# A mixture-of-experts layer tail: each row's two expert outputs ordered by expert number, the first ones loaded and added apart, and the next tile's addition ahead of a tile's norm

## The chip, the cores and the metric

The kernel runs on one core of a Trainium2 chip. The metric is device time in microseconds (us) for one execution of the whole program. The engines that matter here are PE (TensorE, matrix products), DVE (VectorE, elementwise work and statistics), ACT (ScalarE, activations, and the issuer of some DMAs), POOL (GpSimd, the issuer of the gathers and scatters) and SP (SyncE, the issuer of the weight loads).

## The reference, cut to what matters

Two layers. Each ends in a mixture of experts (MoE) over 576 rows (512 prompt rows and 64 sample rows) of width 1024, with 16 experts of which every row uses two:

```
_, idx = lax.top_k(jnp.where(in_grp, sel, NEG_INF), TOP_K)      # TOP_K = 2 experts of a row
w = jnp.take_along_axis(scores, idx, axis=-1)
w = w / w.sum(-1, keepdims=True)
combine = jnp.einsum('tk,tke->te', w, one_hot(idx, N_EXPERTS))
for e in range(N_EXPERTS):
    h = jax.nn.silu(xt @ wg[e]) * (xt @ wu[e])
    y = y + combine[:, e:e + 1] * (h @ wd[e])
...
x = layer_norm(ALPHA * x + y, ln2_g[l], ln2_b[l])               # the layer's end
```

So a row's result is the norm of ALPHA·x plus two weighted expert outputs; which of the two is added first is free.

## The kernel before, in words

The rows lie on chip as five tiles of 128 rows (the last holds 64), `x[128, 5, 1024]`. A loop runs over the two layers. In a layer PE makes the projections (helper `product`, line L1612) in four groups of five tiles, then attention and the spatial gating, the output product, and the MoE.

In the MoE, POOL gathers the rows of an expert from a copy of x in device memory (L644), PE turns and multiplies them (gate and up L1861, down L1884), ACT brings the result out of the banks (`expert_out`, L902), and POOL scatters it to `y2_rows` in device memory (`scatter`, L650), where row 2·r + j holds output j of row r. The scatters stand in the order of the experts, and POOL waits for each to land (L691) before it frees the buffer. Which output is j = 0 is set by `pick1` and `pick2` (L1463 to L1466): `pick1` marks the expert with the best score. From these two VectorE works out the slots (`slot_done`, L1484) that POOL scatters into a table (L670) before it can gather for expert 4 and later.

Weights come as units of 1 MB that SP loads into `raw` (four places) and `raw_far` (two places). Every unit is split: ACT writes its high part (`w_hi`, L423), VectorE the rest (`w_lo`, L429), and each product runs three times over them. The first four units of the next layer are split at the end of a layer.

At the end of a layer ("the tail") ACT waits until both last scatters have landed (`out_free`, L979 to L982), then loads both outputs of each row (L987, L998) into `y_rows`, four tiles of buffers. VectorE goes through the five tiles (L1574 to L1580): add output 0 (L1555), add output 1 (L1558), statistics (L1042, L1044), centre (L1176), and, once ACT has taken the square root (L994), scale and shift (L1182), which marks the tile ready (`x_ready`). In the first layer PE then turns the tile (L1601), ACT and VectorE write its high and low part (`xt_hi` L439, `xt_lo` L444), and PE starts the next layer's first projection on it (`head`, L1639). There PE turns tile t + 1 before it multiplies tile t, and its queue is in order. In the second layer SP stores the tile (L557, L559) and the program ends.

The program has a branch for experts with more than 128 rows (`overflow`); every engine reads the count and jumps past it, as no expert here has so many.

## Time and profile before

| | us |
|---|---|
| median of 3 runs (1206.41 to 1212.07) | 1209.77 |
| the profiled execution | 1211.5 |
| its span in the trace | 1210.0 |
| PE busy | 1066.1 (88%) |
| DVE busy | 904.0 (75%) |
| ACT busy | 699.5 (58%) |
| POOL busy | 188.5 (16%) |

The shares are averages. PE is the bound over most of the span, but in two stretches it stands still: between the layers (about 574 to 634 us it works only in pieces) and after 1162 us, when the last product is done and only the second layer's tail is left. The profile's page has the busy share of PE at 0 in the last of its 40 slices and at 3 tenths in the one before.

### The profile page before, as it was taken

What the parts mean: (1) busy time and instruction counts of PE and PEld (TensorE: products, weight loads), DVE (VectorE), ACT (ScalarE), POOL (GpSimd) and SP (SyncE); (2) the same over time, 40 slices, a digit from 0 to 9 for tenths busy, and PEclk for the clock granted to TensorE, in tenths of its full rate; (3) what the DMA queues carried; (4) which work ended last, traced back from release to release, by engine and by line L of the source; (5) the groups of instructions that cost most, each with busy time, mean ns of one, the idle gap of its engine ahead of it and who ended that gap; (6) DMA issues with size and microseconds to landing.
All of it is one profiled execution on the core that took longest, in us unless ns stands there. A gap on an engine that the chain in (4) does not pass through costs nothing.

```text
span 1210.0 us, 16840 instructions
## 1 busy us (share of the span) xinstructions
PE 1066.1 (88%) x5460; PEld 893.4 (74%) x5460; DVE 904.0 (75%) x1148; ACT 699.5 (58%) x851; POOL 188.5 (16%) x162
## 2 busy tenths in 40 slices
PE   5999799989989999998379988999898999999930
PEld 4987588877878888887269857887677888888820
DVE  2683865388979988886877738655898899888948
ACT  2423665265767887877223247534477888878830
POOL 3000000014522111210020000100173311011100
PEclk9999889998989999999689987999799999999975
DMA  9523101227999999996814202002589999999742
GB/s 293 165 77 105 57 32 44 87 76 275 370 335 380 388 377 380 383 381 259 301 46 155 74 32 87 27 28 95 203 288 379 351 392 391 381 382 389 304 182 83
DMA packets 115748, 273.26 MB, mean 226 GB/s; under 512 B 10144, under 2 KB 13184, under 8 KB 114528
## 3 DMA queue, kind: packets, MB, share of 16 engines
q1 hardware_dynamic: 98608, 227.36, 51.6%
q0 software_dynamic: 14464, 33.01, 7.9%
q10 hardware_dynamic: 2608, 12.06, 2.8%
q8 instruction: 33, 0.54, 0.2%
q14 instruction: 35, 0.29, 0.1%
HBM read 262.02 MB, written 25.22 MB: 237 GB/s over the span
## 4 chain that ended last, share of the span: by engine, by line
PE 55%; DMA 15%; DVE 11%; issue 6%; ACT 5%; DVEq 3%; POOL 3%; ACTq 0%; SPq 0%; POOLq 0%
DMA raw_far<-in_w_gate 10%; PE bankA L1612 9%; PE bankA L1861 8%; PE bankB L1612 7%; PE bankB L1861 6%; PE bankC L1884 4%; PE bankD L1884 4%; PE bankC L1612 4%; PE bankD L1612 4%; POOL slot_rows L670 3%; PE bankG L1685 2%; DVE w_lo L429 2%; PE bankE L1601 2%; ACT w_hi L423 2%; PE bankF L1601 1%
## 5 line engine op out<-in xcount | busy, mean ns | idle before, releaser
L429 DVE TENSOR_TENSOR w_lo<-raw,w_hi 128x2048 fp32r<-128x2048 f32 (+1 forms) x152 | 340.8, 2262 | 61.5 <-ACT w_hi L423 59.5
L423 ACT ACTIVATE w_hi<-raw 128x2048 fp32r<-128x2048 f32 (+1 forms) x152 | 287.1, 1894 | 136.5 <-PE bankC L1612 46.1
L429 DVE TENSOR_TENSOR w_lo<-raw_far,w_hi 128x2048 fp32r<-128x2048 f32 x64 | 146.5, 2288 | 13.7 <-ACT w_hi L423 13.7
L423 ACT ACTIVATE w_hi<-raw_far 128x2048 fp32r<-128x2048 f32 x64 | 122.8, 1918 | 51.0 <-PE bankB L1861 25.0
L1861 PE MATMUL bankB<-w_hi,xe_hi 128*128 128x512 f32 x256 | 103.0, 402 | 1.8 <-DVE w_lo L429 1.8
L1861 PE MATMUL bankA<-w_hi,xe_hi 128*128 128x512 f32 x256 | 102.5, 400 | 1.6 <-DVE xe_lo L444 1.3
L1861 PE MATMUL bankA<-w_lo,xe_hi 128*128 128x512 f32 x256 | 101.5, 397 | 0.0
L1861 PE MATMUL bankA<-w_hi,xe_lo 128*128 128x512 f32 x256 | 101.2, 395 | 0.0
L1861 PE MATMUL bankB<-w_hi,xe_lo 128*128 128x512 f32 x256 | 100.2, 391 | 0.0
L1861 PE MATMUL bankB<-w_lo,xe_hi 128*128 128x512 f32 x256 | 99.8, 390 | 0.0
L650 POOL DMA_INDIRECT y_rows<-expert_out,idx x32 | 47.5, 1485 | 189.6 <-ACT expert_out L902 181.1
L644 POOL DMA_INDIRECT rows<-x_rows,idx x24 | 33.4, 1393 | 223.8 <-PE bankF L1601 160.5
L1861 PEld LDWEIGHTS bankA<-w_hi,xe_hi 128*128 128x128 f32 x256 | 49.1, 192 | 14.9 <-DVE xe_lo L444 4.4
L1884 PE MATMUL bankC<-w_hi,h_hi 128*128 128x512 f32 x128 | 53.4, 417 | 4.8 <-DVE h_lo L444 4.8
L1861 PEld LDWEIGHTS bankA<-w_hi,xe_lo 128*128 128x128 f32 x256 | 49.2, 192 | 10.5
L1861 PEld LDWEIGHTS bankA<-w_lo,xe_hi 128*128 128x128 f32 x256 | 49.2, 192 | 10.0
L1861 PEld LDWEIGHTS bankB<-w_hi,xe_hi 128*128 128x128 f32 x256 | 48.1, 188 | 11.3 <-DVE w_lo L429 2.3
L1861 PEld LDWEIGHTS bankB<-w_hi,xe_lo 128*128 128x128 f32 x256 | 48.0, 188 | 10.6
L1861 PEld LDWEIGHTS bankB<-w_lo,xe_hi 128*128 128x128 f32 x256 | 48.2, 188 | 9.2
L1884 PE MATMUL bankC<-w_hi,h_lo 128*128 128x512 f32 x128 | 50.7, 396 | 0.0
L1884 PE MATMUL bankD<-w_hi,h_hi 128*128 128x512 f32 x128 | 50.6, 395 | 0.0
L1884 PE MATMUL bankC<-w_lo,h_hi 128*128 128x512 f32 x128 | 50.5, 395 | 0.0
(360 smaller groups left out, 2533.3 us busy)
## 6 DMA issues: line engine op xcount, KB each, us to landing
raw<-in_w_up SPq DMA_DIRECT2D x64, 1024.0 KB, 10.7
raw_far<-in_w_gate SPq DMA_DIRECT2D x60, 1024.0 KB, 11.7
raw<-in_w_down SPq DMA_DIRECT2D x60, 1024.0 KB, 11.9
raw<-in_w_in SPq DMA_DIRECT2D x12, 1024.0 KB, 10.0
raw<-in_w_o SPq DMA_DIRECT2D x8, 1024.0 KB, 5.2
y_rows<-y_rows ACTq DMA_DIRECT2D x8, 1024.0 KB, 8.1
x_rows<-x POOLq DMA_DIRECT2D x10, 512.0 KB, 3.0
raw<-in_w_gate SPq DMA_DIRECT2D x4, 1024.0 KB, 8.2
```

The source lines that it names most:

```text
L423: act.activation(w_hi[:, s % RB, :, 0:n], raw_unit(s)[:, :, 0:n], ACT.Copy).then_inc(hi_done, 1)
L429: dve.tensor_tensor(w_lo[:, s % RB, :, 0:n], raw_unit(s)[:, :, 0:n], w_hi[:, s % RB, :, 0:n].bitcast(F32), ALU.subtract).then_inc(lo_done, 1)
L644: pool.indirect_dma_start(out=rows[:, e % 2, :], out_offset=None, in_=x1_dram, in_offset=bass.IndirectOffsetOnAxis(ap=src.bitcast(U32), ax ...
L650: pool.indirect_dma_start(out=y2_dram, out_offset=bass.IndirectOffsetOnAxis(ap=idx[:, e, 0:1].bitcast(U32), axis=0), in_=expert_out[:, e % ...
L670: pool.indirect_dma_start(out=slot_dram, out_offset=bass.IndirectOffsetOnAxis(ap=slots[:, c:c + 1].bitcast(U32), axis=0), in_=ints[:, c, : ...
L1601: ins = pe.transpose(bank_of(name)[:, k * P:(k + 1) * P], src, ident)
L1612: ins = pe.matmul(out, a[:, k, col:col + P], w[:, slot, j, 0:n], start=(m == 0 and a is a_hi and w is w_hi), stop=(m == len(steps) - 1 and ...
L1685: ins = pe.matmul(bank_of(("o", t))[:, h * 64:(h + 1) * 64], probs_t[:, j % 2, 2 * a + b, :], v[b], start=(b == (0 if t else 1)), stop=(b ...
L1861: ins = pe.matmul(out, a[:, 4 * k + t, (c % 2) * P:(c % 2 + 1) * P], w[:, (s + k) % RB, t, :], start=(k == t == 0 and a is xe_hi and w is ...
L1884: ins = pe.matmul(bank_of(f"down{h}")[:, :], a[:, 2 * j + r, cols], w[:, (s + j) % RB, 2 * r + h, :], start=(j == r == 0 and a is h_hi and ...
```

## The change

Five things are changed.

1. `pick1` now marks, for every row, the lower-numbered of its two experts, and `pick2` the other. So every output j = 0 has been scattered once expert 14 is done, as expert 15 can only be a row's second.
2. POOL no longer scatters expert 15 right after expert 14. It first runs the check of `overflow`, and in the branch that is taken here it issues five loads of the outputs j = 0 (`first_outputs`) into `y_first`, which lies over `raw_far`, and then scatters expert 15. The loads wait until every unit of the layer is split.
3. ACT loads only the outputs j = 1 (`y_second`, five buffers), once the last scatter has landed.
4. VectorE adds all five first outputs ahead of the first second output, and adds the second output of tile t + 1, with its statistics, ahead of the centring of tile t.
5. In the first layer, VectorE's part of the split of the next layer's fourth unit (a half-width one) is moved from before the tail to behind it.

```
-                first_max(pick1[:, r * NE:], last_in, NE, desc16, work[:, 0:NE], ma, 1)
+                dve.tensor_tensor(tiles(work[:, 0:NT * NE], NT), tiles(pick[:, 0:NT * NE], NT), over_tiles(desc16, NT), ALU.mult)
+                dve.drain()
+                dve.tensor_reduce(ma, tiles(work[:, 0:NT * NE], NT), AX, ALU.max)
+                dve.drain()
+                dve.tensor_tensor(tiles(pick1[:, :], NT), tiles(work[:, 0:NT * NE], NT), over_experts(ma, NT), ALU.is_equal)
+                dve.drain()
...
-                dve.tensor_tensor(pick2[:, r * NE:], pick[:, r * NE:NT * NE], pick1[:, r * NE:], ALU.subtract)
+                dve.tensor_tensor(pick2[:, :], pick[:, 0:NT * NE], pick1[:, :], ALU.subtract)
...
+                def first_outputs():
+                    hold(lo_done, RX + UNITS * (l + 1))
+                    for t in range(NT):
+                        n = P if t < 4 else DEC
+                        pool.dma_start(y_first[0:n, t, :] if t < 4 else y_first_last[0:n, :],
+                                       y2_dram[2 * P * t:2 * P * t + 2 * n, :].rearrange("(p j) n -> p j n", j=2)[:, 0, :]) \
+                            .then_inc(y_first_in[t], 16)
...
+                def outputs_early():
+                    first_outputs()
+                    send(NE - 1)
...
-                overflow(pool, l, past, block_rows, held_pool)
+                overflow(pool, l, past, block_rows, held_pool, outputs_last, lambda: send(NE - 1), outputs_early)
...
-                for t in range(YB):
+                for t in range(NT):
                     n = P if t < 4 else DEC
...
+                    act.dma_start(y_second[0:n, t, :], y2_dram[2 * P * t:2 * P * t + 2 * n, :]
+                                  .rearrange("(p j) n -> p j n", j=2)[:, 1, :]).then_inc(y_second_in[t], 16)
...
+                def add_first(t):
+                    dve.wait_ge(y_first_in[t], 16 * l + 16)
+                    dve.sem_inc(held_dve, 1)
+                    add_output(t, 0, y_first[:, t, :] if t < 4 else y_first_last[:, :])
+
                 def add_second(t):
...
+                    dve.wait_ge(y_second_in[t], 16 * l + 16)
+                    dve.sem_inc(held_dve, 1)
+                    add_output(t, 1, y_second[:, t, :])
                     dve.drain()
                     row_stats(t).then_inc(var2_done, 1)
...
-                    for s in range(RB):
+                    for s in range(RB - 1):
                         split_lo(dve, l + 1, s)
...
                     for t in range(NT):
-                        add_second(t)
+                        add_first(t)
+                    dve.drain()
...
+                    add_second(0)
+                    for t in range(NT):
+                        if t + 1 < NT:
+                            add_second(t + 1)
+                        centre_2(t)
                         if more and t:
                             rows_lo_x(l + 1, t - 1)
...
                         normalise(t)
                     if more:
                         rows_lo_x(l + 1, NT - 1)
+                        split_lo(dve, l + 1, RB - 1)
```

The first place is POOL's program at the end of the expert loop (`y_rows` names the table of outputs in device memory here, `out_sent0` and `out_sent1` the landing of a scatter). Before, experts 14 and 15 stand one behind the other, and the check follows:

```order
L650 DMA y_rows<-expert_out,idx 1280x1024 [waits freedC,freedD]
L567 ISA
L567 REGISTER_ALU [waits out_sent0]
L650 DMA y_rows<-expert_out,idx 1280x1024 [waits freedC,freedD]
L463 TENSOR_LOAD count_max [waits out_sent1,slot_done]
L463 ISA x2
L464 COMPARE_AND_BRANCH
```

Now the check stands right behind expert 14, and behind its jump come these rows, of which the last DMA is the scatter of expert 15:

```order
L570 ISA
L705 DMA y_first<-y_rows 128x1024 [waits lo_done]
L705 DMA y_first<-y_rows 128x1024 x3
L705 DMA y_first_last<-y_rows 64x1024
L570 REGISTER_ALU
L653 DMA y_rows<-expert_out,idx 1280x1024 [waits freedC,freedD]
L473 UNCONDITIONAL_BRANCH [waits out_sent1]
```

Five loads and the check have moved ahead of the last scatter, on the same queue.

The second place is VectorE's program at the end of the first layer, from the splits for the next layer to the first centring. Before:

```order
L429 TENSOR_TENSOR w_lo<-raw,w_hi 128x4x256
L427 REGISTER_ALU
L429 TENSOR_TENSOR w_lo<-raw,w_hi 128x4x256
L1567 UNCONDITIONAL_BRANCH
L1584 COMPARE_AND_BRANCH
L1554 REGISTER_ALU
L1555 SCALAR_TENSOR_TENSOR x<-y_rows,small,x 128x1024
L1558 SCALAR_TENSOR_TENSOR x<-y_rows,small,x 128x1024
L1042 BN_STATS small<-x 128x6 x2
L1044 BN_AGGR small<-small 128x2
L1176 SCALAR_TENSOR_TENSOR x<-x,small,table 128x1024
```

Now:

```order
L427 TENSOR_TENSOR w_lo<-raw,w_hi 128x4x256
L1591 UNCONDITIONAL_BRANCH
L1621 COMPARE_AND_BRANCH
L1572 SCALAR_TENSOR_TENSOR x<-y_first,small,x 128x1024 x4
L1572 SCALAR_TENSOR_TENSOR x<-y_first_last,small,x 64x1024
L1572 SCALAR_TENSOR_TENSOR x<-y_second,small,x 128x1024
L1059 BN_STATS small<-x 128x6 x2
L1061 BN_AGGR small<-small 128x2
L1572 SCALAR_TENSOR_TENSOR x<-y_second,small,x 128x1024
L1059 BN_STATS small<-x 128x6 x2
L1061 BN_AGGR small<-small 128x2
L1193 SCALAR_TENSOR_TENSOR x<-x,small,table 128x1024
```

Ahead of the first tile's centring there now stand five first additions instead of one, behind the three splits, and the second tile's addition and statistics.

## Rows read from the trace of the kernel before

**Rows 1.** Chain of waits, program's end: start us, us, what.

```profile
1163.09 3.21 DMA y_rows<-expert_out,idx
...
1166.62 4.75 DMA y_rows<-y_rows
```

**Rows 2.** Timeline of DVE, second layer's tail: start, us, engine, line, operation.

```profile
1171.40 1.28 DVE L1555 SCALAR_TENSOR_TENSOR x<-y_rows,small,x 128x1024 f32<-128x1024 f32 x1 [13.62 <-DMA y_rows<-y_rows]
...
1178.44 1.28 DVE L1555 SCALAR_TENSOR_TENSOR x<-y_rows,small,x 128x1024 f32<-128x1024 f32 x1
```

**Rows 3.** POOL at the program's end: timeline, then sequencer by line (ns, first/last start).

```profile
1155.28 0.97 POOL L650 DMA_INDIRECT y_rows<-expert_out,idx  x1 [15.76 <-ACT expert_out L902]
...
L692 POOLq EVENT_SEMAPHORE  x2: 17/17/17, 1158.6 to 1166.4; - x2
...
L589 POOLq ALU_OP  x1: 32/32/32, 1167.4 to 1167.4; - x1
```

**Rows 4.** DMAs by line: ACT's first two, L626 issues, L626's last, POOL's two table loads.

```profile
DMA to landing us min/median/max: 4.8/5.8/6.9
...
L626 POOL DMA_DIRECT2D x_rows<-x x10: 532/548/605, 180.5 to 854.3; - x10
...
DMA to landing us min/median/max: 3.0/3.0/3.0
...
DMA to landing us min/median/max: 5.3/5.9/6.4
```

**Rows 5.** Timeline of DVE, tail of the first layer.

```profile
576.68 6.76 DVE L429 TENSOR_TENSOR w_lo<-raw,w_hi 128x2048 fp32r<-128x2048 f32 x4 [7.33 <-ACT w_hi L423]
583.36 1.28 DVE L1555 SCALAR_TENSOR_TENSOR x<-y_rows,small,x 128x1024 f32<-128x1024 f32 x1
584.73 1.28 DVE L1558 SCALAR_TENSOR_TENSOR x<-y_rows,small,x 128x1024 f32<-128x1024 f32 x1
...
587.77 1.28 DVE L1176 SCALAR_TENSOR_TENSOR x<-x,small,table 128x1024 f32<-128x1024 f32 x1
...
589.20 1.28 DVE L1182 SCALAR_TENSOR_TENSOR x<-x,small,table 128x1024 f32<-128x1024 f32 x1
590.40 1.28 DVE L1555 SCALAR_TENSOR_TENSOR x<-y_rows,small,x 128x1024 f32<-128x1024 f32 x1
...
605.50 0.69 DVE L444 TENSOR_TENSOR xt_lo<-bankE,xt_hi 128x512 fp32r<-128x512 f32 x1 [2.58 <-ACT xt_hi L439]
```

**Rows 6.** Chain of waits, PE between the layers.

```profile
596.13 8.27 PE bankA L1612 x24
...
633.53 5.74 PE bankA L1612 x24
```

**Rows 7.** Timeline of PE: tiles turned between the layers, and one in the MoE.

```profile
609.73 1.11 PE L1601 MATMUL bankE<-ident,x 128*128 128x128 f32 x4 [4.46 <-DVE x L1182]
...
618.72 0.60 PE L1601 MATMUL bankE<-ident,x 128*128 128x128 f32 x4
...
626.14 0.65 PE L1601 MATMUL bankE<-ident,x 128*128 128x128 f32 x4 [0.90 <-DVE x L1182]
...
342.88 1.11 PE L1601 MATMUL bankE<-ident,rows 128*128 128x128 f32 x4 [3.39 <-DMA rows<-x_rows,idx]
```

**Rows 8.** Stretches: us, busy of PE, PEld, DVE, ACT, POOL, PEclk, DMA, GB/s.

```profile
609.70:618.70 9.00, 8.97 (x32) 7.53 (x33) 8.59 (x11) 1.49 (x3) 0.00 (x0) 0.69 0.01 2
```

**Rows 9.** Timeline of DVE, first layer, ahead of the slots.

```profile
290.09 0.17 DVE L1321 TENSOR_REDUCE r<-in_group 128x1 f32<-128x16 f32 x1
...
291.68 0.23 DVE L1464 TENSOR_SCALAR pick<-pick,consts 128x16 f32<-128x16 f32 x1
...
292.54 0.23 DVE L1474 TENSOR_TENSOR work_wide<-rcol,pick 128x80 f32<-128x80 f32 x1
```

**Rows 10.** Timeline, DVE and POOL, a scatter in the MoE.

```profile
530.98 4.49 DVE L429 TENSOR_TENSOR w_lo<-raw,w_hi 128x2048 fp32r<-128x2048 f32 x2
...
531.91 2.22 POOL L650 DMA_INDIRECT y_rows<-expert_out,idx  x1 [15.90 <-ACT expert_out L902]
```

More of the change, by code:

```diff
@@ L202, in build @@
         hidden = over(base_m, "hidden", [P, 2, HALF], at=2 * QB + 8 * HALF)
-        y_rows = over(base_m, "y_rows", [P, YB, 2, D])
+        y_first = over(base_t, "y_first", [P, NT - 1, D], at=8192)
+        y_first_last = over(base_m, "y_first_last", [P, D])
+        y_second = over(base_m, "y_second", [P, NT, D], at=8 * HALF)
         before, ones, iota = consts[:, 0:P], consts[:, P:2 * P], consts[:, 2 * P:3 * P]
@@ L321, in build @@
         out_free = [sem("out_free0"), sem("out_free1")]
-        y_in = [sem(f"y_in{i}") for i in range(YB)]
-        y_used = sem("y_used")
+        y_first_in = [sem(f"y_first_in{t}") for t in range(NT)]
+        y_second_in = [sem(f"y_second_in{t}") for t in range(NT)]
         stores = sem("stores")
@@ L453, in build, with overflow @@
         PE_STEPS, ACT_STEPS, DVE_STEPS = 7, 11, 12
-        def overflow(eng, l, past, body, apart, close=None):
+        def overflow(eng, l, past, body, apart, close=None, begin=None, otherwise=None):
             eng.wait_ge(slot_done, l + 1)
@@ L464, in overflow @@
             with eng.If(most > P):
+                if begin is not None:
+                    begin()
                 ran0 = eng.snap(past, min_val=0, max_val=DEPTH * OVB)
@@ L471, in overflow @@
                 eng.reg_add(past, past, OVB)
+            if otherwise is not None:
+                with eng.Else():
+                    otherwise()
         def new_past(eng):
@@ L683, in gather_next, with send @@
                     gather(e, idx[:, e, 1:2])
-                for e in range(NE):
-                    if e + 4 < NE:
-                        gather_next(e + 4)
+                def send(e):
                     for c in range(2):
@@ L692, in _, with outputs_last @@
                     pool.sem_inc(out_free[e % 2], 1)
+                for e in range(NE - 1):
+                    if e + 4 < NE:
+                        gather_next(e + 4)
+                    send(e)
+                def first_outputs():
[5 more added lines that the diff above has]
+                            .then_inc(y_first_in[t], 16)
+                def outputs_last(ran):
+                    first_outputs()
+                def outputs_early():
+                    first_outputs()
+                    send(NE - 1)
                 def block_rows(e, b, ran):
@@ L1517, in _ @@
                 dve.tensor_tensor(w12[:, :, 0], s1, srec, ALU.mult)
-                dve.tensor_tensor(w12[:, :, 1], s2, srec, ALU.mult).then_inc(w12_done, 1)
+                dve.tensor_tensor(w12[:, :, 1], s2, srec, ALU.mult)
                 def block_dve(e, b, ran):
@@ L1573, in tail, with centre_2 @@
                     dve.sem_inc(held_dve, 1)
+                    dve.wait_ge(scaled, l + 1)
+                    dve.sem_inc(held_dve, 1)
+                    dve.drain()
                     for t in range(NT):
-                        add_second(t)
+                        add_first(t)
+                    dve.drain()
+                    def centre_2(t):
+                        dve.drain()
+                        centre(t, table[:, 0:2, :])
+                    add_second(0)
+                    for t in range(NT):
+                        if t + 1 < NT:
+                            add_second(t + 1)
+                        centre_2(t)
                         if more and t:
                             rows_lo_x(l + 1, t - 1)
-                        dve.drain()
-                        centre(t, table[:, 0:2, :])
                         normalise(t)
```

29 lines of the change are left out of this document (6 added, 23 removed).

## The prediction

> **What bounds the kernel now.** The page comes first: PE is busy 88% of the span, but not in the stretch between the layers and not at the end. The chain of waits at the end says what runs there instead: the last scatter takes 3.21 us from its issue at 1163.09, ACT's first load of outputs is issued at 1166.62 and takes 4.75 us [rows 1], and from 1171.40 VectorE alone works through five tiles. The timeline gives its step: from the first addition of one tile to that of the next 7.04 us [rows 2], so the last tile is ready at 1171.4 + 5 × 7.04 = 1206.6. Between the layers VectorE does the same chain with the splits ahead of it [rows 5], and PE restarts on it [rows 6, 7]. These two tails are what the change touches; a third place, the slot work in the middle of each layer, is touched by a handful of small instructions [rows 9].
>
> The sum is made against the profiled execution, 1211.5 us (span 1210.0 and 1.5 around it), which lies 1.7 above the median of 1209.77.
>
> **End of the program.** An addition with its drain takes 584.73 − 583.36 = 1.37 us [rows 5], so without the first one a tile's step is 5.67 and five take 28.35. The second output of the next tile only changes places with a centring, so it alters the order and not the sum; ACT's root stands in no gap of VectorE there now, so hiding it gains nothing. What decides is when the second outputs are there.
>
> POOL had expert 14 landed by 1158.6, and from such a landing to the first instruction behind the check's jump it took 1166.4 to 1167.4, 1.0 us [rows 3]. So the first loads are issued from 1159.6, five at 0.55 [rows 4], until 1162.4: the last scatter's issue at 1163.09 stays. A lone transfer of 512 KB on this queue landed 3.0 us after its issue [rows 4]: the first one at 1162.6. For the others I have two rates: ACT's first two loads of 1 MB were issued 0.45 apart and landed at 4.8 and 6.9, so about 2.5 us for 1 MB and 1.25 for 512 KB; POOL's two table loads were issued 0.53 apart and landed at 5.3 and 6.4, so 1.64 each [rows 4]. I take 1.25, since those rows read the same table of outputs: four and a half transfers are through at 1162.6 + 3.5 × 1.25 = 1167.0 (1168.3 by the other rate). The last scatter stands behind them on POOL's queue. No row shows whether it must wait for their data. I take that it does: 1167.0 + 1.25 = 1168.2 instead of 1166.3; the ends are 1166.3 (beside them) and 1168.3 + 1.64 = 1169.9. On this point the Trainium skill (DMA: Bandwidth & Descriptors, "SWDGE vs HWDGE vs iDMA") says that only one queue is allocated to the software path; that leans to the wait, and no run here shows it.
>
> ACT issues 0.32 later, and 512 KB land in 4.75 − 1.25 = 3.5: the second outputs' tail starts at 1172.1 (1170.1 to 1173.8) against 1171.40. The five first additions end 1.3 behind the last first load, by 1168.3, so they are hidden; they would cost if those loads came after 1170. The end: 1172.1 + 28.35 = 1200.4, a gain of 6.1 (8.1 to 4.4).
>
> **Between the layers.** Here the first additions are not hidden, since they stand behind the splits in VectorE's order, and the splits wait for ACT: VectorE stood idle for 7.33 us ahead of them and still does [rows 5]. The four splits took 6.76 from 576.68; without the half-width fourth (1.15) VectorE is free at 582.2. Five additions at the back-to-back step of 1.20 (589.20 to 590.40) and a drain bring it to 588.3, where the second addition of tile 0 begins; before it began at 584.73 [rows 5]. The loads are there: they need about 1.9 us more than before and are wanted 3.6 later. Then two tiles' second additions and statistics (3.04 each, 584.73 to 587.77) precede the first centring: 594.4 against 587.77. So tile 0 is ready 6.6 later, and the projection of tile 0, which in both orders follows one tile's additions and a low part, starts at 602.6 instead of 596.13 [rows 6].
>
> PE then takes back a part, as it stood still for 4.46 and 0.90 us later on [rows 7]. Its projection of tile 0 takes 8.27 [rows 6] to 610.8; the low part of tile 1 follows at 611.9 (605.50 against 604.40 before), and as tile 2 is by then added and centred, it is ready 2.8 us later, at 614.7 (before 609.6). PE has again waited, some 3.2 us. After a wait of 3.39 its four transposes took 1.11 instead of 0.60 us [rows 7], the lower of its two levels (1.2 against 2.4 GHz), and the stretch behind the wait of 4.46 has a granted clock of 0.69 [rows 8]. So I take the same 9.0 us from turning tile 2 to turning tile 3 (609.73 to 618.72), not the 6.5 of the next step (618.72 to 625.24): tile 3 at 623.8, tile 4 at 630.3, and there is no further wait, as VectorE is done with tile 4 by 628. Before, tile 4 was turned at 626.14. From there to the last projection at 633.53 nothing changes. Cost: 4.2. At the higher clock it is 2.1; if PE never catches up it is 6.5. The moved split (1.15) lands behind tile 4 on VectorE while PE multiplies tiles 3 and 4 (11 us), and PE needs it only in the next group: nothing.
>
> **Slots.** Five small steps, 290.09 to 291.68, become three of the 0.31 us that the 80-wide form takes (292.54 [rows 9] and its successor): 1.59 less 0.93 is 0.66 per layer. But five steps of the narrow form should not have taken 1.59, so a part of it is a stall that may stay. I take 0.25 per layer, 0.5 in all; nothing if the gathers behind it wait for bandwidth, 1.3 if all of it goes.
>
> **Sum.** −6.1 + 4.2 − 0.5 = −2.4: 1209.1 in the profile's terms, 1207.4 as a median.
>
> **A rule that speaks against it.** A scatter's issue took 2.22 us while VectorE subtracted one part of a weight from another, both in SBUF [rows 10], against 0.97 beside an idle VectorE [rows 3]. The Trainium skill (SBUF — State Buffer, "Who interferes with whom") has it that a VectorE instruction with two SBUF inputs contends with a GpSimd instruction that reads SBUF and holds the port to its end; the trace agrees, with the 2.22. The first additions have two SBUF inputs and fall on the last scatter. By the rule its issue ends 1.25 later, which changes nothing where the scatter waits for the loads' data anyway, and takes 1.25 off the rival that follows.
>
> **Rivals.** *The scatter is not held by the loads in front of it.* For it: no row shows one transfer of this queue held by another's data. Against it: the two table loads, issued 0.53 apart, landed 1.64 apart [rows 4]. The tail starts at 1170.1, and the sum is −8.1 + 4.2 − 0.5 = −4.4, a median of 1205.4; if PE also keeps its higher clock between the layers, −6.5 and 1203.3. *PE restarts late and cold and never catches up.* It keeps the 6.5 us of tile 0 and falls to its lower clock once more ahead of tile 3 (9.0 instead of 6.5, 2.5 more): +9.0, and with −6.1 and −0.5 it is slower by 2.4, a median of 1212.2. It decides from the point at which PE waits over 3 us ahead of tile 3 as well; for it speaks that every wait of that length here was followed by the lower clock, against it that VectorE has tile 3 ready at 614.7 + 3.04 + 1.2 + 1.3 + 1.5 = 621.7 (addition and statistics, centring, low part, scale), before PE can take it. *The first loads do not come early*: they land at the price of the tables (5.3, then 1.64 each), the last at 1170.6, the scatter behind them at 1172.2, the tail at 1176.0: a gain of 2.2 only, and with 4.2 and 0.5 the sum is +1.5, a median of 1211.3.
>
> **How the numbers follow.** Forecast 0.50, scatter beside the loads 0.27 (a third of it with PE at its higher clock), PE late 0.13, late loads 0.10. Measurement tells about 0.5%, 6 us, from no change. Only the last part of the first rival reaches that on the fast side, and the spread of the runs (1206.4 to 1212.1) adds some: faster 0.15. None of the slow cases reaches it alone; both together with the spread, 0.08. Same: 0.77. The unknown costs at their ends give −8.1 + 2.1 − 1.3 = −7.3 and +2.4, so 1202.5 to 1212.2, and with the spread of a median 1202 to 1213.
>
> **What would show it.** At the end: the last tile's scale and shift ending near 1200, five additions on VectorE between 1163 and 1169, the last scatter landing 5 us after its issue instead of 3.2. Between the layers: tile 0 turned near 597, PE's projection of it near 602.6, tile 4 near 630. I am wrong if the scatter's issue itself moves by more than 1 us, if VectorE waits for a second output in the middle of a tail, or if PE turns tile 4 before 627 or after 633.

## The result, and the profile after

The changed kernel is slower. Its median is 1215.49 us over 14 runs (1212.57 to 1225.99), against 1209.55 for the kernel before over 14 runs (1205.18 to 1216.51): a ratio of 1.0055 with a 95% interval of 1.0035 to 1.0075. The profiled execution took 1212.95 us (span 1211.3), and so lies 2.5 below its median, while that of the kernel before (1211.5) lay 2.0 above its own. The pair of profiles therefore shows 1.3 us (by their spans) of a difference that is about 6.6 by the ratio and 5.9 between the medians.

The end of the program first. The chain of waits of the changed kernel there, which answers to [rows 1, 2]:

```profile
1154.68 3.24 DMA y_rows<-expert_out,idx
...
1160.02 1.70 POOL y_first L705 x4
1162.17 0.59 POOL y_first_last L705
...
1163.06 11.54 DMA y_rows<-expert_out,idx
1174.84 4.64 DMA y_second<-y_rows
1179.62 1.28 DVE x L1572
...
1206.69 1.28 DVE x L1199
```

The loads are issued where they were expected, and the last scatter is issued at 1163.06 (before 1163.09; counted from expert 14's scatter it is 8.4 us instead of 7.8). But it lands 11.5 us after its issue instead of 3.2, ACT's first load takes 4.64, and the second additions start at 1179.62 instead of 1171.40. From there to the last scale and shift it is 28.35 us, as forecast. How long the loads took stands with their lines (POOL's five loads, then ACT's five):

```profile
DMA to landing us min/median/max: 4.8/8.8/11.3
...
DMA to landing us min/median/max: 4.6/7.0/9.5
```

VectorE's timeline shows the same from its side. The figure in brackets is the idle time ahead of a row: it waits for three of the five loads, and then 4.05 us for the first second output.

```profile
1164.93 2.51 DVE L1572 SCALAR_TENSOR_TENSOR x<-y_first,small,x 128x1024 f32<-128x1024 f32 x2 [7.74 <-DMA y_first<-y_rows]
1170.07 1.28 DVE L1572 SCALAR_TENSOR_TENSOR x<-y_first,small,x 128x1024 f32<-128x1024 f32 x1 [2.62 <-DMA y_first<-y_rows]
1173.09 1.28 DVE L1572 SCALAR_TENSOR_TENSOR x<-y_first,small,x 128x1024 f32<-128x1024 f32 x1 [1.74 <-DMA y_first<-y_rows]
...
1179.62 1.28 DVE L1572 SCALAR_TENSOR_TENSOR x<-y_second,small,x 128x1024 f32<-128x1024 f32 x1 [4.05 <-DMA y_second<-y_rows]
```

Between the layers, the timeline of VectorE in the changed kernel, which answers to [rows 5]:

```profile
576.09 5.63 DVE L427 TENSOR_TENSOR w_lo<-raw,w_hi 128x2048 fp32r<-128x2048 f32 x3 [7.34 <-ACT w_hi L421]
581.93 4.87 DVE L1572 SCALAR_TENSOR_TENSOR x<-y_first,small,x 128x1024 f32<-128x1024 f32 x4 [0.21 <-issue]
586.72 1.27 DVE L1572 SCALAR_TENSOR_TENSOR x<-y_first_last,small,x 64x1024 f32<-64x1024 f32 x1
590.12 1.28 DVE L1572 SCALAR_TENSOR_TENSOR x<-y_second,small,x 128x1024 f32<-128x1024 f32 x1 [2.13 <-DMA y_second<-y_rows]
```

That of PE, where tiles 0, 2, 3 and 4 are turned [rows 7], and the chain with the first and the last projection of the group and the turning of tile 4 between them as the chain has it [rows 6]:

```profile
598.86 1.11 PE L1638 MATMUL bankE<-ident,x 128*128 128x128 f32 x4 [26.32 <-DVE x L1199]
...
615.53 0.65 PE L1638 MATMUL bankE<-ident,x 128*128 128x128 f32 x4 [3.08 <-DVE x L1199]
...
622.37 0.65 PE L1638 MATMUL bankE<-ident,x 128*128 128x128 f32 x4 [0.28 <-DVE x L1199]
...
628.77 0.60 PE L1638 MATMUL bankE<-ident,x 128*128 128x128 f32 x4
```

```profile
604.36 7.22 PE bankA L1649 x24
...
628.93 0.45 PE bankE L1638 x4
...
636.05 4.15 PE bankA L1649 x17
```

**Stretches.** To compare many profiles I cut the span at POOL's instructions, which stand in every kernel: the first layer's third gather (A), the scatter of expert 14 in the first layer (B), the first gather of the second layer (C), the scatter of expert 14 in the second layer (D), and the end. B and C of before, and of after:

```profile
566.85 0.97 POOL L650 DMA_INDIRECT y_rows<-expert_out,idx  x1 [15.83 <-ACT expert_out L902]
...
859.79 1.09 POOL L644 DMA_INDIRECT rows<-x_rows,cur_src  x1 [3.83 <-DVE cur_src L1427]
```

```profile
566.24 0.97 POOL L653 DMA_INDIRECT y_rows<-expert_out,idx  x1 [15.83 <-ACT expert_out L924]
...
861.18 1.10 POOL L647 DMA_INDIRECT rows<-x_rows,cur_src  x1 [3.48 <-DVE cur_src L1444]
```

B to C is 292.94 and 294.94. All profiles, in us; the last column is when tile 4 was turned, counted from B:

| kernel | start-A | A-B | B-C | C-D | D-end | tile 4 |
|---|---|---|---|---|---|---|
| before | 285.6 | 281.3 | 292.9 | 295.5 | 54.7 | 59.3 |
| before, again | 283.9 | 282.3 | 290.4 | 294.2 | 54.8 | 58.7 |
| slots alone | 286.9 | 280.3 | 291.4 | 297.1 | 54.7 | 58.7 |
| last layer alone | 290.7 | 279.8 | 290.1 | 293.9 | 57.3 | 58.6 |
| last layer alone, again | 288.7 | 282.3 | 291.3 | 296.0 | 56.0 | 59.2 |
| last layer, SP, apart | 283.7 | 281.0 | 289.7 | 294.4 | 51.0 | 58.4 |
| after | 287.0 | 279.3 | 294.9 | 293.5 | 56.6 | 62.5 |
| after, again | 288.9 | 279.2 | 298.5 | 294.3 | 56.0 | 62.2 |
| first loads on SP | 285.5 | 279.2 | 295.3 | 295.5 | 52.7 | 62.5 |
| scatter first | 286.5 | 282.6 | 302.8 | 295.3 | 59.5 | 68.0 |
| half width | 282.4 | 280.4 | 298.5 | 295.5 | 51.8 | 59.9 |
| table apart | 286.8 | 282.3 | 297.7 | 295.7 | 53.4 | 62.9 |
| table apart, SP | 289.1 | 282.5 | 295.5 | 296.7 | 50.0 | 60.7 |
| first layer alone | 286.9 | 279.1 | 299.6 | 295.9 | 54.9 | 64.6 |
| no next tile ahead | 285.7 | 279.1 | 298.6 | 294.9 | 55.1 | 61.5 |
| adds ahead of splits | 288.6 | 281.8 | 292.4 | 296.0 | 50.5 | 59.3 |

D to the end follows the tail's form closely: 54.7 to 54.9 for the old one, 56.0 to 57.3 for the new one as it was written. B to C is 289.7 to 292.9 (mean 291.0) in the six kernels with the old first tail and 294.9 to 299.6 (mean 297.1) in the seven that have VectorE's new order and the loads ahead of the scatter (after, after again, first loads on SP, half width, both with the table apart, first layer alone). So by the profiles the loss is about 1.6 at the end and 6.2 between the layers.

In some of the expectations below, 51.3 us are named for the end of the kernel before: these count from the landing of expert 14's scatter, the 54.7 of the table from its issue. Ratios are to the kernel before as it was timed in the same set; its medians there were 1208.5, 1210.1, 1212.5 and 1212.0 us.

### The profile page after: what moved, and what is told of

It reads as the page before. It is cut to its first block, busy times and chain, and to the rows that moved or that the text cites. A ratio compares the mean times of both kernels' runs of the same rounds, so it can differ in the third digit from the quotient of the medians.

```text
span 1211.3 us, 16852 instructions
## 1 busy us (share of the span) xinstructions
PE 1054.7 (87%) x5460; PEld 884.4 (73%) x5460; DVE 903.4 (75%) x1144; ACT 699.1 (58%) x851; POOL 192.5 (16%) x172
## 4 chain that ended last, share of the span: by engine, by line
PE 55%; DMA 17%; DVE 10%; issue 6%; ACT 4%; DVEq 3%; POOL 3%; POOLq 0%; ACTq 0%; SPq 0%
DMA raw_far<-in_w_gate 10%; PE bankA L1649 9%; PE bankA L1898 8%; PE bankB L1649 7%; PE bankB L1898 6%; PE bankC L1649 4%; PE bankD L1649 4%; PE bankC L1921 4%; PE bankD L1921 3%; POOL slot_rows L673 3%; PE bankG L1722 3%; DMA y_rows<-expert_out,idx 2%; DVE w_lo L427 2%; PE bankE L1638 2%; ACT w_hi L421 2%
## 5 line engine op out<-in xcount | busy, mean ns | idle before, releaser
L1898 PEld LDWEIGHTS bankA<-w_hi,xe_lo 128*128 128x128 f32 x256 | 48.0, 188 | 10.1
```

Source lines behind the costliest of these rows:

```text
L1898: ins = pe.matmul(out, a[:, 4 * k + t, (c % 2) * P:(c % 2 + 1) * P], w[:, (s + k) % RB, t, :], start=(k == t == 0 and a is xe_hi and w is ...
```

## The experiments

**Once more.** The changed kernel, unaltered.

> The changed kernel once more, unaltered, for a second profile of it. In its first profile (1212.95 us) the last scatter landed 11.5 us after its issue instead of 3.2, the second outputs' additions began at 1179.6 and the tail was then 28.35 long. Its 14 times lie between 1212.6 and 1226, much wider than before's. Theory A (the loads on POOL's queue are slow by an amount that varies, and the last scatter stands behind them): if this run is slower than 1214, the difference sits between the last scatter's issue and its landing (over 12.5 us in the second layer or over 10.4 in the first), and the stretches between stay as they were. Rival B (the loss is in PE's restart between the layers): the scatter lands within 1 us of 11.5 again, and the difference sits between 580 and 640 us.

It took 1218.56 us. The last scatter landed 11.1 us after its issue, the end was half a microsecond shorter (56.0), the first tail the same to 0.3 us (tile 4 at 62.2 after B). Neither theory is met: the 5.6 us more sit elsewhere, 1.8 ahead of B and 3.6 behind the projections, in attention. There the granted clock differs. PE's busy time (second figure) and granted clock (third from the end) in two stretches of 10 us, of before and then of this run:

```profile
795.00:805.00 10.00, 8.66 (x46) 7.42 (x47) 3.73 (x7) 3.06 (x8) 0.00 (x0) 1.00 0.11 44
805.00:815.00 10.00, 10.00 (x74) 9.21 (x72) 5.11 (x9) 2.58 (x5) 0.00 (x0) 1.00 0.00 0
```

```profile
795.00:805.00 10.00, 8.43 (x43) 7.24 (x42) 3.94 (x9) 3.69 (x9) 0.61 (x1) 0.75 0.14 54
805.00:815.00 10.00, 10.00 (x37) 8.21 (x36) 0.86 (x2) 0.00 (x0) 0.00 (x0) 0.74 0.00 0
```

In both, a wait of PE of 1.57 us for VectorE's `mt_lo` (the low part of another operand) ends in the first stretch, before and then in this run:

```profile
796.34 0.50 PE L1612 MATMUL bankA<-w_hi,mt_hi 128*128 128x512 f32 x1 [1.57 <-DVE mt_lo L444]
```

```profile
798.43 0.50 PE L1649 MATMUL bankA<-w_hi,mt_hi 128*128 128x512 f32 x1 [1.57 <-DVE mt_lo L442]
```

In this run that wait is followed by some 10 us at the lower level, 1.2 GHz, in which PE gets half as much done.

**First loads on SP.**

```
+            def first_outputs(n_layers):
+                for sm, v in ((out_sent[1], 16 * (n_layers * (NE // 2) - 1)), (out_sent[0], 16 * n_layers * (NE // 2)),
+                              (lo_done, RX + UNITS * n_layers)):
+                    sp.wait_ge(sm, v)
...
-                        pool.dma_start(y_first[0:n, t, :] if t < 4 else y_first_last[0:n, :],
+                    sp.dma_start(y_first[0:n, t, :] if t < 4 else y_first_last[0:n, :],
...
+                        if s == RB:
+                            with sp.If(l > 0):
+                                first_outputs(1)
...
+            first_outputs(DEPTH)
```

> The five loads of first outputs are issued by SP, on the queue of the weight loads, once scatter 14 has landed; the last scatter then has POOL's queue to itself. Theory A (POOL's queue moves such loads slowly and holds the scatter behind them): the loads, issued from about 1158.5 to 1161, are through by 1167, the last scatter lands 3.2 to 4.5 us after its issue at 1163, the second outputs' additions begin at 1171 to 1172.5 instead of 1179.6, and the end is 7 to 8.5 earlier; in the first layer the second outputs are added from about 588 instead of 590.1. The whole: 8 to 11 below the changed kernel in the profile, a median of 1202 to 1206, a ratio to the kernel before of 0.994 to 0.997. Rival C (rows of 4 KB out of a table that is still being written are slow on any queue): the loads still need 8 to 11 us and the scatter 8 or more, and the time stays within 2 us of 1215. Rival B (the restart of PE between the layers is the loss): the end gains its 7 us, but tile 4 is turned later than 628 as well, and the time stays above 1209.5.

A ratio of 1.0052 (1.0033 to 1.0072). The chain at the end:

```profile
1163.37 8.37 DMA y_rows<-expert_out,idx
1171.96 4.55 DMA y_second<-y_rows
1176.65 1.28 DVE x L1582
```

and SP's issue of the first four loads, from its timeline (D is at 1155.58 here):

```profile
1159.01 3.04 SPq L523 DMA_DIRECT2D y_first<-y_rows  x4
```

D to the end is 52.7, 3.6 less than in the mean of the changed kernel's two profiles: the scatter is issued 0.6 sooner behind D and lands 3.0 sooner after its issue, but still takes 8.4 with a queue to itself. Not all of the 3.6 is the queue: SP's first load goes out 3.4 us behind D, POOL's went out 5.3 behind it (1160.02), as POOL makes its check first. So 1.9 of the 3.6 go with the earlier issue. From the first load's issue to the scatter's landing it is 12.7 us here and 14.4 in the mean of the two, but 13.1 to 14.6 in all five profiles with POOL's loads in this form (no next tile ahead and the last layer alone are the others), so of the 1.7 that is left no more than 0.4 stands clear of that spread. And the scatter lands 0.9 us behind the last load here (1171.7; 1162.10 + 8.7 = 1170.8) as it landed 1.2 behind it on one queue (1174.6; 1173.4): what it waits for is mainly the loads' bytes, whichever queue they stand in. Theory A's numbers are missed, and rival C's are met (8.4, 1214.6). The timed gain is smaller, 0.4 us by the two ratios; their intervals together allow up to 3.8.

**Scatter first.**

```
-                    first_outputs()
-                    send(NE - 1)
+                    send(NE - 1, first_outputs)
```

The loads are issued between the scatter and POOL's wait for it.

> The loads stay on POOL's queue but are issued behind the last scatter. Theory A: the scatter lands 3.2 to 4.2 us after its issue at 1163.1 again, since nothing stands ahead of it; the loads, issued from 1164.1 to 1166.3, land as slowly as before, the last one 9 to 12 us after its issue, at 1175 to 1178; the second outputs, loaded by ACT from 1166.7, are there first, so VectorE waits for first outputs and the second additions begin at 1176 to 1179.5: 0 to 3 us better than the changed kernel at the end, a ratio of 1.002 to 1.006 to the kernel before. Rival D (the scatter is slow because VectorE's first additions and its descriptors want the same port): the additions now come after its issue, so it is quick as well, but the loads are quick too (through by 1171) and the second additions begin by 1173. Rival C (bytes out of the table are slow on any queue): ACT's loads are slow too (over 9 us for the first).

1.0155 (1.0129 to 1.0181), the worst. The scatter lands in 3.3 us again; the price moves to the loads:

```profile
1175.01 0.97 POOL y_rows L653
1175.98 2.17 POOL y_first L707 x4
1178.16 15.25 DMA y_first_last<-y_rows
1193.54 1.28 DVE x L1573
```

POOL's loads and ACT's now share the engines, and the last one lands 15.3 us after its issue. That the scatter's 11.5 us is the loads ahead of it is shown; rival D (the port) falls, since the loads are no quicker. I had expected 0 to 3 us of gain; with both heaps of loads under way together the second additions come later still, and so does the first layer's tail (tile 4 at 68.0).

**Half width.** Half of the columns of the first outputs are not loaded and not added.

```
-                        pool.dma_start(y_first[0:n, t, :] if t < 4 else y_first_last[0:n, :],
+                        pool.dma_start(y_first[0:n, t, 0:HALF] if t < 4 else y_first_last[0:n, 0:HALF],
```

> The loads on POOL's queue and the first additions take only the first 512 of the 1024 columns, so half of the first outputs is left out of the sum: the same number of pieces, each 2 KB instead of 4. Theory A, if the queue is slow by bytes: the loads land at about half the spacing, the last scatter 6 to 7.5 us after its issue instead of 11.5, the second additions begin near 1175. If the queue is slow by pieces: the scatter lands 11 to 12 after its issue as before. Rival D (the port, held by the first additions): the scatter gains with the shorter additions only, 2 us or less.

The scatter lands 6.6 us after its issue (expected by bytes 6 to 7.5), D to the end is 51.8. The cost goes with the bytes, not with the number of pieces, which is unchanged.

**Table apart.**

```
-            ints[:, 2 * t + j, 0] = 2 * (t * P + np.arange(P)) + j
+            ints[:, 2 * t + j, 0] = j * ROWS + t * P + np.arange(P)
...
-                                       y2_dram[2 * P * t:2 * P * t + 2 * n, :].rearrange("(p j) n -> p j n", j=2)[:, 0, :]) \
+                                       y2_dram[P * t:P * t + n, :]) \
...
+                    act.dma_start(y_second[0:n, t, :], y2_dram[ROWS + P * t:ROWS + P * t + n, :]).then_inc(y_second_in[t], 16)
```

> The table of outputs is laid out as all outputs j = 0, then all outputs j = 1, so that a tile's load reads 512 KB in one piece instead of every other 4 KB; the loads stay on POOL's queue ahead of the last scatter. Theory C (the gaps between the pieces make the loads slow): first loads at 350 GB/s or more from the second microsecond on, the last one 6 to 7.5 us after its issue instead of 11.2, the last scatter 5 to 8 us after its issue, the second additions at 20 to 21 us behind expert 14's scatter instead of 24.9; ACT's five loads through in 7.5 us instead of 9.5. Theory A (POOL's queue): as the changed kernel, scatter 10 to 12 us after its issue, only ACT's loads may gain.

D to the end 53.4, 3.0 less. The scatter lands 9.8 us after its issue, so theory C too holds for a part only and theory A's forecast is the nearer one (10.0 to 11.5 in the five profiles with the mixed table on POOL's queue); the clear effect is on ACT's loads, 3.20 for the first instead of 4.64:

```profile
1170.82 9.76 DMA y_rows<-expert_out,idx
1180.81 3.20 DMA y_second<-y_rows
```

**Both.** The last two edits together.

> The changed kernel with its first outputs loaded by SP (as in the second run) and the table laid out as all outputs j = 0, then all j = 1. The end, from expert 14's scatter, took 56.6 us in the changed kernel, 52.7 with SP's loads, 53.4 with the table apart, 54.7 before. If the two add up: 49.5 to 51; the last scatter lands 4 to 6 us after its issue. Between the layers nothing is mended by either (298 us from expert 14's scatter to the next layer's first gather in the mean of the seven profiles with a new first tail, 291 in the three with an old one), so the whole is level with the kernel before or up to 4 us behind it: a ratio of 1.000 to 1.004. If the end gains and the ratio stays over 1.005, the part between the layers is larger than 6 us.

1.0010 (0.9981 to 1.0040), as expected; the scatter lands 6.9 us after its issue (4 to 6 expected). D to the end is 50.0: 6.3 less than in the mean of the changed kernel's two profiles, where the two edits alone gave 3.6 and 3.0. What the engines moved while the first loads ran (DMA's busy share and GB/s are the last two figures), in the changed kernel, and here:

```profile
1162.00:1164.00 2.00, 0.00 (x0) 0.00 (x0) 0.00 (x0) 1.49 (x2) 1.70 (x3) 0.97 1.00 221
1164.00:1166.00 2.00, 0.00 (x0) 0.00 (x0) 1.06 (x1) 0.00 (x0) 0.10 (x1) 0.50 0.97 356
1166.00:1168.00 2.00, 0.00 (x0) 0.00 (x0) 1.45 (x2) 0.00 (x0) 0.00 (x0) 0.50 0.98 178
```

```profile
1169.00:1171.00 2.00, 1.15 (x6) 0.61 (x4) 0.00 (x0) 1.02 (x2) 0.00 (x0) 1.00 0.98 334
1171.00:1173.00 2.00, 0.00 (x0) 0.00 (x0) 0.66 (x1) 1.49 (x2) 0.97 (x1) 1.00 1.03 397
```

The same busy share moves 178 to 356 GB/s in the one and 334 to 397 in the other: a busy engine is not a full one. Both edits are in this difference; no stretch of it is told apart by edit.

**One layer alone.** The new tail in the second layer only, then in the first only (there `outputs_late` and `outputs_soon` change places). `outputs_soon` is the change's order on POOL, `outputs_late` scatters expert 15 without loads; ACT and VectorE keep the loads and the order of the kernel before in the other layer.

```
                 def outputs_early():
+                    with pool.If(l < DEPTH - 1):
+                        outputs_late()
+                    with pool.If(l > DEPTH - 2):
+                        outputs_soon()
```

> The new tail in the second layer alone: in the first layer the outputs are loaded by ACT in pairs once both last scatters have landed, added tile by tile, and all four splits stand ahead of them, as in the kernel before; the slot work is the changed one. From expert 14's scatter to the end the changed kernel took 53.3 and 52.7 us in its two profiles, the kernel before 51.3. Theory E (the loss has two places: 1.5 to 2 at the end, and the rest between the layers, where the restart costs 3 and in some runs a stretch of TensorE's lower clock near 800 us another 3.5): this kernel is 1.0 to 2.0 us behind the kernel before, a ratio of 1.0005 to 1.002, and its times spread no wider than those of before. Rival G (the wide spread and most of the loss come from something in the second layer): a ratio over 1.003.

> The reverse: the new tail in the first layer alone, the second layer's tail as before (pairs of outputs loaded once both last scatters have landed). Theory E: the end takes 51.3 us from expert 14's scatter again; between the layers 2 to 3 us are lost, and 3.5 more in the runs with a stretch of the lower clock near 800 us; a ratio of 1.002 to 1.005 with times over 1214 among them. Rival G: within 0.1% of the kernel before, and as narrow.

Last layer alone 1.0069 (1.0047 to 1.0092), first layer alone 1.0088 (1.0059 to 1.0118). The stretches split as expected: B to C 290.1 with D to the end 57.3, and 299.6 with 54.9. But both times are 2 to 6 us worse than these stretches say, and together they exceed the whole change: by its time the first run meets rival G (over 1.003), by its stretches theory E. The first of them again:

> The new tail in the second layer alone, once more, for a second profile: the first (1213.3 us) was the fastest of its six runs, so it does not show where the others lost 4 us more. Theory E: the first layer's part to the next first gather stays at 290 to 293 us from expert 14's scatter, and the loss is in the end (57 us or more from expert 14's scatter, with the last scatter landing 11 us or later after its issue). Rival H (stretches of the lower clock come at random in either layer's attention): a stretch under 0.7 in 200 to 235 us or in 795 to 840 us, and the end at 56 to 57.5.

1215.8 us, B to C 291.3, the end 56.0, the scatter landing 10.1 us after its issue: theory E's loss at the end (57 us or more) isn't there, and what is left over sits in the first stretch, start to A, 288.7 and 290.7 against 285.6 and 283.9 in the two profiles of before, where no edit reaches. In it the lower clock stands behind the same 1.57 us wait for `mt_lo`, between 180 and 240 us, in both (6.8 and 10.2 us of it, none in the two of before). Rival H is borne out for these two profiles. The timed runs lean the same way: an estimate from their mean granted clock (what it lacks to 1, doubled, times the span) gives 151 us at the lower level in the six runs with the last layer alone and 142 in the eleven of the kernel before timed beside them, which at half speed is 4.5 of the 7 us between them. Up to 1.5 of that is PE standing idle in the longer end. Why the kernel before met it less often in those comparisons isn't settled.

**Before, again.**

> The kernel before once more, unaltered, for a second profile: its first one (1211.5) lies 3 us above the median of its times here (1208.5), while that of the changed kernel lay 2.5 below its own. Theory E: from expert 14's scatter in the first layer to the first gather of the second 291 to 294 us as in the first profile (292.9), from expert 14's scatter to the end 51.3, no stretch of the lower clock near 800 us; where it differs from 1211.5, the difference sits ahead of 566 us or among the experts of the second layer. Rival: the kernel before has such a stretch as well, and 296 us or more.

1207.23 us, B to C 290.4 (291 to 294 expected), the end 54.8, no lower clock near 800 us: theory E but for 0.6 us.

**Slots alone.**

```
-                first_max(pick1[:, r * NE:], last_in, NE, desc16, work[:, 0:NE], ma, 1)
+                dve.tensor_tensor(tiles(work[:, 0:NT * NE], NT), tiles(pick[:, 0:NT * NE], NT), over_tiles(desc16, NT), ALU.mult)
...
```

> The kernel before with the slot work alone changed (outputs ordered by expert number, three wide steps instead of five narrow ones); both tails as before. In the profiles of the changed kernel the steps from the third gather (286.97) to the fifth (336.13) took 49.16 instead of 49.53 us. Theory E (the loss sits in the tails and in TensorE's lower clock behind the first one): 0.2 to 0.6 us gained per layer, a ratio of 0.9985 to 1.0. Rival S (something that all the variants so far share, the slot work or the order of the outputs among them, costs 3 to 5 us, as the last layer's tail alone came out 0.7% behind while its profile showed 1.8 us): a ratio of 1.002 or more.

1.0005 (0.9978 to 1.0033): neither a gain nor a cost that can be told. The interval (−2.7 to +4.0 us) leaves out the 5 us of rival S, but not its 3.

**The end mended, the first tail as before.**

```
+            first_outputs(DEPTH)
...
+            ints[:, 2 * t + j, 0] = j * ROWS + t * P + np.arange(P)
```

This is the kernel with the new tail in the last layer alone, with SP's loads behind the loop over the layers and with the table apart. POOL scatters expert 15 right behind expert 14 again, ahead of the check, here and in the first of the next two runs.

> The second layer's tail alone is new (the first layer's as before), with the two mends that shortened the end: the first outputs loaded by SP, the table laid out as all j = 0, then all j = 1. From expert 14's scatter to the end 50.0 us were measured with these two together, 54.8 in the kernel before, 56 to 57.3 with POOL's loads out of the mixed table; between the layers 290 to 293 as with every old first tail. Theory E (end and first tail account for the loss): 4 to 5 us faster than the kernel before, a ratio of 0.995 to 0.998. Rival S (a kernel with a new tail in the second layer alone carries 4 us more that its profiles do not show): a ratio of 0.999 to 1.002.

0.9981 (0.9950 to 1.0012), median 1209.42 against 1211.96. It is faster than the changed kernel by its ratio (the intervals don't touch), and likely, not surely, than the kernel before: the interval holds theory E's 0.998 and rival S's 1.000. The end is 51.0, B to C 289.7:

```profile
1156.58 7.30 DMA y_rows<-expert_out,idx
...
1164.32 3.24 DMA y_second<-y_rows
```

**Order on VectorE.** First, first additions ahead of the splits and no next tile ahead, with both mends; then the changed kernel with the last hunk alone, the next tile's addition put back. In both, ACT also writes a tile's high part (`xt_hi`) ahead of the next tile's root again, as in the kernel before. The change had swapped these two, so that ACT takes the next root first, a sixth difference that the list of the change leaves out.

```
+                for t in range(NT):
+                    add_first(t)
+                dve.drain()
                 with dve.If(l < DEPTH - 1):
                     for s in range(RB - 1):
...
-                    add_second(0)
                     for t in range(NT):
-                        if t + 1 < NT:
-                            add_second(t + 1)
+                        add_second(t)
                         centre_2(t)
```

> Both tails new, with SP's loads and the table apart; in addition the five first additions stand ahead of the splits, in the 7.3 us in which VectorE waits for ACT, and no next tile's addition stands ahead of a centring any more. Theory E (the loss between the layers is the first additions and the next tile's addition in front of the first centring): the loads land 7 to 12 us behind expert 14's scatter, the additions end at 13, the splits at 18.6, and the second additions begin there instead of at 23.9; tile 0 is turned at about 24.5 us behind expert 14's scatter (23.8 in the kernel before, 32.6 in the changed one), tile 4 2 to 4 us earlier than before; from expert 14's scatter to the next layer's first gather 288 to 292, the end 50. A ratio of 0.993 to 0.998. Rival B2 (PE's restart suffers from the delayed splits instead): tile 0 turned after 28 us, 294 or more, a ratio of 0.999 or more.

> The changed kernel, but a tile's second addition stands ahead of its own centring only, not the next tile's. By the changed kernel's rows an addition with its statistics takes 2.86 us (590.12 to 592.98). Theory E: tile 0 is turned 2.9 us earlier, at 29.7 us behind expert 14's scatter instead of 32.6, PE's projection of it starts 2.9 earlier and PE waits for tiles 1 and 2 instead; the last of the five projections comes at most 1 us earlier. At the end the tail is 28.35 long as before. Rival: VectorE stalls for ACT's root between the additions, and the tail is 1 us or more longer.

The first is at 1.0009 (0.9985 to 1.0033). Its loads come later than I took, so the additions end 15.5 behind B and delay the splits:

```profile
578.71 3.78 DVE L1572 SCALAR_TENSOR_TENSOR x<-y_first,small,x 128x1024 f32<-128x1024 f32 x3 [5.74 <-DMA y_first<-y_rows]
583.47 1.28 DVE L1572 SCALAR_TENSOR_TENSOR x<-y_first,small,x 128x1024 f32<-128x1024 f32 x1 [0.98 <-DMA y_first<-y_rows]
...
586.19 5.63 DVE L427 TENSOR_TENSOR w_lo<-raw,w_hi 128x2048 fp32r<-128x2048 f32 x3 [0.25 <-issue]
591.74 1.28 DVE L1572 SCALAR_TENSOR_TENSOR x<-y_second,small,x 128x1024 f32<-128x1024 f32 x1
```

Tile 0 is turned at 27.1 (32.6 in the changed kernel, 23.8 before), tile 4 at 59.3, and B to C is 292.4, 4.7 less than the mean of the seven and 1.4 more than that of the old tail. The profile to set it against is that of both mends, which has the same loads and table: tile 0 at 30.7, tile 4 at 60.7, B to C 295.5. VectorE's order is worth 3.6 at tile 0 and 1.4 at tile 4 against it; the rest of the 3.1 in B to C falls behind the projections, where that profile has 3.4 us of the lower clock and this one none. So the order causes most of tile 0's delay; how much of the loss in B to C goes back to it isn't shown by one profile. The forecast ratio of 0.993 to 0.998 was missed. In the second (1214.96 us) tile 0 is turned at 29.5, which the addition with its statistics explains to 0.2 us, and tile 4 at 61.5, 1.0 earlier; VectorE stalls for nothing. But PE waits again ahead of tile 2, and B to C is 298.6, within the range of the seven: putting the next tile's addition ahead costs about 1 us up to tile 4, not 3, and no gain is seen behind it.

## Why the prediction was wrong, point by point

**The end** (−6.1 forecast, +1.6 measured, as the mean of two profiles of each kernel). This is the step that failed. Right were the issue of the loads (1160.02 for 1159.6), of the scatter, and the tail of 28.35. Wrong was the sentence "I take 1.25, since those rows read the same table of outputs". Those rows [rows 4] read the table in pairs of pieces, 8 KB at a time, by ACT. The new loads read every other 4 KB, and POOL issues them: the first landed at 1164.8, not 1162.6, and the last at 1162.17 + 11.2 = 1173.4, so 3.5 transfers took 8.6, or 2.5 each, which is outside my upper rate of 1.64. The scatter did wait behind them, as I had chosen, but landed at 1174.6 instead of 1168.2; ACT's first load took 4.64 for 3.5. These are 6.4 and 1.1, the whole of the 7.5 between 1179.6 and 1172.1. The runs split it: 3.6 for SP's queue with its earlier issue and 3.0 for the table's layout, by one profile each, and 50.0 us from D to the end with both mended, near the 48.6 forecast.

On the queue: the same loads moved from POOL to SP shorten the end by 3.6 us, of which 1.9 go with their earlier issue; the 1.7 that is left is hardly clear of the spread. The Trainium skill (DMA: Bandwidth & Descriptors, "Issuing engines are not separate DMA queues") has it that transfers from any issuing engine run on the same 16 engines, and that issuing from several saves only the issue time, usually little; the trace agrees for the larger part of the 3.6, and in that the scatter waited for the loads from either queue (8.4 us with them on SP's), though the 1.9 us were not little here.

On the layout: 4 KB out of every 8 KB took 4.64 us where the same bytes in one piece took 3.20. The Trainium skill (DMA: Bandwidth & Descriptors, "Latency and other measured facts") tells of slow copies for rows a large power of two apart, from 512 KiB on; whether this is the same effect at 8 KB, no run shows.

The rule of the port, which the prediction set against itself, was not tried in the changed kernel: the scatter's issue took 1.04 us, but VectorE's first addition began at 1164.93, when it was over.

The late-loads rival took the price of the tables (5.3, then 1.64 each) and was the right kind, but it still left a gain of 2.2.

**Between the layers** (+4.2 forecast, 2.1 to 6.5). The mechanism held: the first additions stand behind the splits and are not hidden, and tile 0 was turned at 598.9 (597 forecast), its projection at 604.4 (602.6). The 1.8 came from "The loads are there": ACT's first load waited for the delayed scatter, and VectorE for it, 2.13 us. PE took it back later: ahead of tile 2 it waited 3.08 us and yet kept the higher clock (0.65 for the four transposes; 6.8 us on to tile 3, where 9.0 were forecast), so tile 4 was turned at 62.5 behind B, 3.2 later than before; the seven profiles have 3.4 more than the six with the old tail. That is inside the range. The clock there was luck: the same 3.08 us stand ahead of tile 2 in all ten profiles with VectorE's first additions in this layer, and the higher clock stayed behind it in three (after, after again, both mends) and fell in seven, as with the first loads on SP:

```profile
612.97 1.11 PE L1648 MATMUL bankE<-ident,x 128*128 128x128 f32 x4 [3.08 <-DVE x L1209]
```

What I left out came after: "From there to the last projection at 633.53 nothing changes" is true, but attention follows. There the lower clock stood near 230 us behind B in five of the seven profiles and in none of the six, 4.9 us of it in the mean, which at half speed is 2.4 lost. With 3.4 it makes 5.8 of the 6.2. That it comes with the new tail is seen; why isn't shown. Behind the same wait in the first layer, ahead of every edit, it also comes and goes, in 11 of 14 profiles of the other kernels and in none of the two of before.

**Slots** (−0.5): in the first layer's trace the three steps take 1.29 us (291.51 to 292.80) where the five took 1.59, so 0.30 is gained for the 0.25 forecast; the stall of 0.43 stayed. The time can't tell it, as the run with slots alone says.

**The sum.** +1.6 and +6.2 are 7.8 by the profiles, about 6.6 by the times, where −2.4 was forecast; 7.7 of the 10.2 between 7.8 and −2.4 are the end's. Of the signs that I had named, VectorE's waits at the end (4.05 us for a second output ahead of the tail, not in its middle) and the scatter's 11.5 us instead of 5 showed the failure; tile 4 at 628.93 was within the bounds of 627 to 633. That every wait of over 3 us is followed by the lower clock did not hold: of the ten waits of 3.08 us ahead of tile 2 three were not.

## What to carry to other kernels

A transfer's rate is to be taken from a row of the same queue and the same pattern in memory, not of the same table: half of every 8 KB from POOL's queue cost twice what whole 8 KB rows from ACT's did. Before a load is put ahead of a transfer on which the end depends, count its bytes into that transfer's time, on another queue too (8.4 us instead of 3.2 with the loads on SP's), and lay out what is read in halves as halves. Early additions gain only where the engine idles when their data land; here the idle time was over before the loads were in.

## What had not been expected of the hardware

DMA engines at a busy share of 0.98 moved 178 GB/s, and at 1.03 397, in two kernels that differ in the layout and in the queue. And one wait of PE, 1.57 us long and at the same place of the program, is in some runs followed by 3 to 10 us at 1.2 GHz and in others by none, which at half speed moves the whole time by 2 to 5 us from run to run; a single pair of profiles (1.3 us apart here) doesn't show a difference of 0.5%.
